# Attention in twelve steps instead of sixteen: two query blocks share a step in a two-block transformer kernel

## The chip, the cores and the metric

The kernel runs on one core of one Trainium2 chip. Times are device microseconds (us) of one execution. TensorE is written PE (its weight loads PEld), VectorE DVE, ScalarE ACT, GpSimd POOL, SyncE SP.

## What is computed

Two transformer blocks follow each other on 512 tokens of width 1024, in float32. There are three attentions, each with 8 heads of width 64: A (chunked, with a relative bias) and B (stick-breaking) in the first block, F (forgetting) in the second. Cut to what the change touches:

```python
# A: softmax over keys of (q.k * scale + bias), mask by chunks of 64
scores = einsum('bnqhd,bnkhd->bnhqk', qc, kb) * (dh ** -0.5)
probs = softmax(where(valid, scores + bias, -inf));  out = probs @ vb
# B: per query block of 128, causal
log_keep = where(causal, -softplus(z), 0.0)
log_after = lax.cumsum(log_keep, axis=3, reverse=True) - log_keep
w = where(causal, exp(log_sigmoid(z) + log_after), 0.0);  out = w @ vh
# F: per query block of 128, causal
s = q @ k.T * scale + c[:, :, t0:t1, None] - c[:, :, None, :t1]
out = softmax(where(mask, s, -inf)) @ v
```

Around them stand the projections, gates, a gated feed-forward in each block and some smaller pieces. Query block qb (0 to 3, 128 queries each) sees the first qb + 1 key blocks of 128: its scores are 128, 256, 384 or 512 columns wide.

## The kernel before

**The projections** are the bulk. Every weight matrix is read in slots of 128 rows by 512 columns. SP loads a slot into `w_raw`, ACT copies it to a rounded `w_hi` (L862), POOL makes the rest `w_lo` (L661), eight slots ahead of PE, and PE multiplies it: 4 tiles of 3 matmuls of 512 columns each (L1650). A group is 4 or 8 slots (k) that add up in banks 0 to 3, one bank for each tile. At a group's last slot the tiles end one after the other, and each is then *taken* out of its bank, mostly by DVE (`take_dve`, such as L1118 for kB, L1123 for a gate, L1136 for branchA and branchH). The next group's first slot waits for that, tile by tile (`tile_taken`).

**Attention** runs between slots on banks 4 to 7. Heads go in four pairs; a pair had four steps, one for each query block, so a branch had STEPS = 16. Each branch also has LAG = 2 steps more, and one after them. Step i is issued by each engine at its own place in one common list, SCHEDULE, which is walked by every engine in the same order. In step i

- PE (`att_pe`) makes the scores of step i for both heads into banks 4 and 5 (L1560), if a pair is finished its 16 products with the values into bank 6 (L1575, 'PV'), and the transposes of the probabilities of step i - 2 into banks 6 and 7 (L1587), two for each key block.
- DVE (`att_dve`) for A and F makes the reciprocal of step i - 1, then waits until the transposes of step i - 2 are through, since the scores' copy in `work` goes into the buffer that they read (`ring_free`), and then, for each head, adds the mask (F: L1222), adds the bias and finds the maximum (A: L1212, F: L1224, 'reduce'). Each of these is linked: the next waits for its end. Last it copies transposes out of their banks (L1231; A both units, B and F the first, ACT the second at L782).
- for B, DVE makes the reverse cumulative product of step i - 1 (L1189, 'scan', after a memset of one column) and adds the mask (L1206), ACT makes two sigmoids for each head (L770, L771), and POOL multiplies the two (L709).
- ACT (`att_act`) for A and F scales the probabilities of step i - 1 (L761) and makes the exponentials (L779).

Where the steps stand is computed by `attention(kind, first, last)` in `make_schedule`: step i gets a share of the slots first to last in proportion to `room`, which was block + 5. A step stands behind its slot, and behind the take of a group if that slot is the group's last. Here 'gateH1.6' means group 1 of gateH behind its slot 6 (slots count from 0), and A9 is step 9 of attention A.

Of the kernel before, what the change touches and what calls it, by code (L numbers as in the profile page):

```python
# [23 lines left out]
P = 128  # L24
# [17 lines left out]
STEPS = TB * PAIRS  # L42
# [72 lines left out]
def make_schedule():  # L115
# [90 lines left out]

def transposed(i):

    if not 0 <= i < STEPS:
        return ()  # L210
    return (1,) if i % TB < 2 else (0, 1)
# [108 lines left out]
def two_block_kernel(nc, a, out):  # L320
    ctx = ExitStack()
    with ctx:
# [326 lines left out]
        def _(e):  # L649
# [25 lines left out]
            for x in SCHEDULE:  # L675
# [60 lines left out]
        def transposes_out(e, kind, i, unit, copy):  # L736

            a_, c = A[kind], i % TB + 1
            pair, q = i // TB, slice((c - 1) * P, c * P)
# [4 lines left out]
            if c <= 2:  # L744
                o = probs_t[kind][:, :, 0:c, q]
                copy(o, ps[b][:, 0:2 * c * P].rearrange("p (h c t) -> p h c t", h=2, c=c)).then_inc(bank_free[b], 1)
            else:
                o = probs_t[kind][:, unit, 0:c, q]
                copy(o, ps[b][:, 0:c * P].rearrange("p (c t) -> p c t", c=c)).then_inc(bank_free[b], 1)

        def att_act(e, kind, i):

            a_ = A[kind]
            n = (i % TB + 1) * P
            if 1 <= i <= STEPS and kind != "B":
# [18 lines left out]
            elif i < STEPS:  # L774
                k = 0 if kind == "A" else 1
                for j in (2 * i, 2 * i + 1):
                    ring = work[j % 4][:, 0:n]
                    e.wait_ge(a_["s_ready"], j + 1)
                    e.activation(ring, ring, ACT.Exp, scale=-1.0,  # L779
                                 bias=mneg[:, k, j:j + 1], accum_out=rsum[:, k, j:j + 1]).then_inc(a_["e_ready"], 1)  # L780
# [392 lines left out]
        def att_dve(e, kind, i, link):  # L1173

            a_ = A[kind]
            n = (i % TB + 1) * P
            if finished_pair(i - 1) is not None:
                outputs_rest(e, kind, finished_pair(i - 1), link)
            if 1 <= i <= STEPS and kind == "B":
                m = ((i - 1) % TB + 1) * P  # L1180
                for h in range(2):
                    j = 2 * i - 2 + h
                    e.wait_ge(a_["keep_ready"], j + 1)
                    if i > 1:
                        e.wait_ge(a_["p_ready"], j - 1)
                    k_, o_ = keep[h], after[h]
                    link(e.memset(o_[:, m - 1:m], 1.0))
                    rev = lambda t, lo_, hi_: t[:, hi_ - 1:(lo_ - 1 if lo_ else None):-1]
                    e.tensor_tensor_scan(rev(o_, 0, m - 1), rev(k_, 1, m), rev(k_, 1, m), 1.0,  # L1189
                                         ALU.mult, ALU.bypass).then_inc(a_["after_ready"], 1)  # L1190
            elif 1 <= i <= STEPS:
                k = 0 if kind == "A" else 1
                e.wait_ge(a_["e_ready"], 2 * i)
                e.reciprocal(rinv[:, k, 2 * i - 2:2 * i], rsum[:, k, 2 * i - 2:2 * i]).then_inc(a_["r_ready"], 1)
            if i < STEPS:
                if kind != "B":
                    ring_free(e, kind, i)
                for h in range(2):
                    j = 2 * i + h
                    head = 2 * (i // TB) + h  # L1200
                    ring = work[j % 4]
                    b, use = USE[("sc", kind, j)]
                    e.wait_ge(a_["sc_done"], j + 1)
                    if kind == "B":
                        d = ps[b][:, n - P:n]
                        e.tensor_tensor(d, d, strict[:, :], ALU.add).then_inc(a_["s_ready"], 1)  # L1206
                    elif kind == "A":
                        if j == 0:

                            e.wait_ge(bias_full, 16)  # L1210
                            link(e.tensor_scalar(bias_mask[64:128, :, S - 64:S], bias_mask[64:128, :, S - 64:S], NEG, None, ALU.add))
                        link(e.tensor_tensor_reduce(out=ring[:, 0:n], in0=ps[b][:, 0:n], in1=bias_mask[:, head, S - n:S],  # L1212
                                                    scale=-1.0, scalar=3e38, op0=ALU.add, op1=ALU.min,
                                                    accum_out=mneg[:, 0, j:j + 1]))
                        e.nop().then_inc(bank_free[b], 1)
                        e.nop().then_inc(a_["s_ready"], 1)
                    else:

                        if j == 0:
                            e.wait_ge(ff["rows"], 16)  # L1220
# [321 lines left out]
        def att_pe(e, kind, i):  # L1542
# [3 lines left out]
            if i < STEPS:  # L1546
                pair, qb = divmod(i, TB)
# [8 lines left out]
                n = (qb + 1) * P  # L1556
                banks = [bank_wait(e, ("sc", kind, 2 * i + h)) for h in range(2)]
                for h in range(2):
                    r = slice(64 * h, 64 * h + 64)
                    e.matmul(banks[h][:, 0:n], qk1[qn][r, pair, qb * P:n], qk1[kn][r, pair, 0:n],  # L1560
                             start=True, stop=True).then_inc(a_["sc_done"], 1)
            pair = finished_pair(i)
            if pair is not None:
# [4 lines left out]
                last = TB * pair + TB - 1  # L1568
# [323 lines left out]
```

## Time and profile before

| | us |
|---|---|
| median of 3 runs | 1579.41 (1578.83 to 1580.74) |
| the profiled execution | 1579.64 |
| its span, first to last instruction | 1577.9 |
| PE busy | 1565.9 (99%) |
| POOL busy | 754.7 (48%) |
| ACT busy | 693.4 (44%) |
| DVE busy | 642.9 (41%) |

The span is what the profile shows between the first and the last instruction; 1.7 us of the execution lie around it. A matmul's busy time overlaps that of the next, so what a matmul costs is read from the starts: one start to the next. The three attentions lie at 93 to 193 us (A), 200 to 316 us (B) and 971 to 1088 us (F).

### The profile page before, as it was taken

What the parts mean: (1) busy time and instruction counts of PE and PEld (TensorE: products, weight loads), DVE (VectorE), ACT (ScalarE), POOL (GpSimd) and SP (SyncE); (2) the same over time, 40 slices, a digit from 0 to 9 for tenths busy, and PEclk for the clock granted to TensorE, in tenths of its full rate; (3) what the DMA queues carried; (4) which work ended last, traced back from release to release, by engine and by line L of the source; (5) the groups of instructions that cost most, each with busy time, mean ns of one, the idle gap of its engine ahead of it and who ended that gap; (6) DMA issues with size and microseconds to landing.
All of it is one profiled execution on the core that took longest, in us unless ns stands there. A gap on an engine that the chain in (4) does not pass through costs nothing.

```text
span 1577.9 us, 23446 instructions
## 1 busy us (share of the span) xinstructions
PE 1565.9 (99%) x8030; PEld 1256.7 (80%) x8030; DVE 642.9 (41%) x1075; ACT 693.4 (44%) x1196; POOL 754.7 (48%) x585
## 2 busy tenths in 40 slices
PE   8999999999999999999999999999999999999999
PEld 7876777788888888888877887768888888888887
DVE  5334356444355444220477543543342122210234
ACT  5555455433544444332543644655453333322342
POOL 6632365644644554444578434323544444444441
PEclk9999999999999999999999999999999999999999
DMA  5422222223323333333232323222333333332331
GB/s 184 143 80 61 74 74 60 75 81 87 112 83 99 106 100 93 100 100 88 80 88 76 93 69 132 69 67 74 101 94 100 100 93 100 107 100 94 97 96 61
DMA packets 103352, 145.60 MB, mean 92 GB/s; under 512 B 11109, under 2 KB 57166, under 8 KB 103134
## 3 DMA queue, kind: packets, MB, share of 16 engines
q1 hardware_dynamic: 103102, 142.30, 30.3%
q10 hardware_dynamic: 160, 2.11, 0.3%
q8 instruction: 55, 0.90, 0.2%
q14 instruction: 35, 0.29, 0.1%
HBM read 142.24 MB, written 2.13 MB: 91 GB/s over the span
## 4 chain that ended last, share of the span: by engine, by line
PE 95%; DVE 2%; ACT 1%; issue 1%; POOL 1%; DMA 1%; SPq 0%; DVEq 0%; ACTq 0%; POOLq 0%
PE bank L1650 86%; PE bank L1560 2%; PE bank L1587 2%; PE bank L1575 2%; POOL w_lo L661 1%; DMA xtok<-in_x 0%; PE bank L1805 0%; PE bank L1636 0%; ACT L869 0%; PE bank L1828 0%; PE bank L1845 0%; ACT hE L1046 0%; PE bank L1781 0%; PE bank L1839 0%; PE bank L1866 0%
## 5 line engine op out<-in xcount | busy, mean ns | idle before, releaser
L661 POOL TENSOR_TENSOR w_lo<-w_raw,w_hi 128x512 fp32r<-128x512 f32 x516 | 695.7, 1357 | 782.2 <-ACT w_hi L862 781.5
L862 ACT ACTIVATE w_hi<-w_raw 128x512 fp32r<-128x512 f32 x516 | 319.0, 628 | 651.1 <-PE bank L1650 579.1
L1650 PE MATMUL bank<-h_hi,w_lo 128*128 128x512 f32 x1244 | 490.0, 394 | 0.8 <-ACT hv L981 0.7
L1650 PE MATMUL bank<-h_hi,w_hi 128*128 128x512 f32 x1244 | 484.6, 390 | 0.0
L1650 PE MATMUL bank<-h_lo,w_hi 128*128 128x512 f32 x1244 | 484.1, 389 | 0.0
L1650 PEld LDWEIGHTS bank<-h_hi,w_lo 128*128 128x128 f32 x1244 | 233.5, 188 | 51.1 <-issue 2.3
L1650 PEld LDWEIGHTS bank<-h_hi,w_hi 128*128 128x128 f32 x1244 | 233.5, 188 | 49.3
L1650 PEld LDWEIGHTS bank<-h_lo,w_hi 128*128 128x128 f32 x1244 | 233.7, 188 | 46.9
L1245 DVE TENSOR_TENSOR bank<-bank,rstd 128x512 f32<-128x512 f32 x88 | 60.1, 700 | 261.6 <-PE bank L1650 261.6
L1650 PE MATMUL bank<-g_hi,w_lo 128*128 128x512 f32 x352 | 137.0, 389 | 0.0
L1650 PE MATMUL bank<-g_hi,w_hi 128*128 128x512 f32 x352 | 136.9, 389 | 0.0
L1650 PE MATMUL bank<-g_lo,w_hi 128*128 128x512 f32 x352 | 136.9, 389 | 0.0
L1144 DVE TENSOR_TENSOR xT<-bank,xT 128x512 f32<-128x512 f32 x32 | 22.0, 688 | 206.5 <-PE bank L1650 204.5
L1650 PEld LDWEIGHTS bank<-g_hi,w_hi 128*128 128x128 f32 x352 | 66.1, 188 | 13.8
L1650 PEld LDWEIGHTS bank<-g_hi,w_lo 128*128 128x128 f32 x352 | 66.1, 188 | 13.7
L1650 PEld LDWEIGHTS bank<-g_lo,w_hi 128*128 128x128 f32 x352 | 66.1, 188 | 13.6
L1650 PE MATMUL bank<-w_lo,h_hi 128*128 128x512 f32 x184 | 73.6, 400 | 0.4 <-DVE fk L1118 0.4
L1650 PE MATMUL bank<-w_hi,h_hi 128*128 128x512 f32 x184 | 71.9, 391 | 0.0
L1650 PE MATMUL bank<-w_hi,h_lo 128*128 128x512 f32 x184 | 71.7, 390 | 0.0
L1254 DVE SCALAR_TENSOR_TENSOR acc<-bank,vec,acc 128x511 f32<-128x511 f32 x88 | 62.9, 746 | 13.2 <-ACT acc L817 8.1
L779 ACT ACTIVATE work<-work,mneg 128x128 f32<-128x128 f32 (+3 forms) x64 | 36.0, 562 | 32.7 <-DVEq L1228 17.1
L1650 PE MATMUL bank<-mix_hi,w_hi 128*128 128x512 f32 x128 | 49.8, 389 | 0.0
(297 smaller groups left out, 1781.0 us busy)
## 6 DMA issues: line engine op xcount, KB each, us to landing
w_raw<-in_w_in SPq DMA_DIRECT2D x168, 256.0 KB
w_raw<-in_w_ffn_up SPq DMA_DIRECT2D x88, 256.0 KB
w_raw<-in_w_ffn_down SPq DMA_DIRECT2D x88, 256.0 KB
w_raw<-in_w_ffn_gate SPq DMA_DIRECT2D x88, 128.0 KB
w_raw<-in_w_ffn_up SPq DMA_DIRECT2D x88, 128.0 KB
w_raw<-in_w_out SPq DMA_DIRECT2D x32, 256.0 KB
w_raw<-in_w_branch_a SPq DMA_DIRECT2D x16, 256.0 KB
w_raw<-in_w_branch_b SPq DMA_DIRECT2D x16, 256.0 KB
```

The lines of the kernel that those rows point to most:

```text
L661: e.tensor_tensor(w_lo[:, pos % SPLIT_SLOTS, :], w_raw[:, pos % RAW_SLOTS, :], w_hi[:, pos % SPLIT_SLOTS, :].bitcast(F32), ALU.subtract).t ...
L779: e.activation(ring, ring, ACT.Exp, scale=-1.0, bias=mneg[:, k, j:j + 1], accum_out=rsum[:, k, j:j + 1]).then_inc(a_["e_ready"], 1)
L862: e.activation(w_hi[:, pos % SPLIT_SLOTS, :], w_raw[:, r, :], ACT.Copy).then_inc(hi_full, 1)
L1144: e.tensor_tensor(xT[:, j, :], bank, xT[:, j, :], ALU.add).then_inc(x_ready, 1)
L1245: e.tensor_tensor(ps[banks + n][:, :], ps[banks + n][:, :], rstd[:, :], ALU.mult).then_inc(q["scaled"], 1)
L1254: e.scalar_tensor_tensor(out=o, in0=ps[banks + n][:, 0:S - shift], scalar=vec[:, conv_col(tap, col, n // 2)], in1=o, op0=ALU.mult, op1=ALU ...
L1560: e.matmul(banks[h][:, 0:n], qk1[qn][r, pair, qb * P:n], qk1[kn][r, pair, 0:n], start=True, stop=True).then_inc(a_["sc_done"], 1)
L1575: mm = e.matmul(bank[64 * h:64 * h + 64, c * P:S], vtok[vn][:, c, d], probs_t[kind][:, h, c, c * P:S], start=c == 0, stop=c == TB - 1, ski ...
L1587: mm = e.transpose(bank[:, o:o + P], work[(2 * j + h) % 4][:, c * P:(c + 1) * P], ident[:, :])
L1650: mm = e.matmul(ps[banks + n][:, :], l, r, start=k == 0 and i == 0, stop=k == p.kc - 1 and i == 2)
```

## The change

Query blocks 0 and 2 of a pair of heads now go in one step, of 128 + 384 = 512 columns in one bank; blocks 1 and 3 go alone. The order in a pair is block 1, blocks 0 and 2, block 3. A branch has 12 steps. What DVE and ACT did once for a head and a block is still done for each piece in A and F; the semaphores count steps. In B the sigmoids and POOL's product go over both pieces in one instruction, and the scans stay one for each piece. The `room` of the three kinds of step is 6, 9 and 8, over the same slots first to last.

```diff
-STEPS = TB * PAIRS
+BLOCKS = ((1,), (0, 2), (3,))
+PARTS = len(BLOCKS)
+STEPS = PARTS * PAIRS
...
-        room = [min(i, STEPS - 1) % TB + 5 for i in range(STEPS + LAG + 1)]
+        room = [(6, 9, 8)[min(i, STEPS - 1) % PARTS] for i in range(STEPS + LAG + 1)]
...
+def pieces(i):
+
+    at, said = 0, []
+    for qb in BLOCKS[i % PARTS]:
+        said.append((qb, at, (qb + 1) * P))
+        at += (qb + 1) * P
+    return said
+
+
+def width(i):
+    return sum(n for _, _, n in pieces(i))
...
-    return (1,) if i % TB < 2 else (0, 1)
+    return (1,) if width(i) <= 2 * P else (0, 1)
...
-                    link(e.memset(o_[:, m - 1:m], 1.0))
-                    rev = lambda t, lo_, hi_: t[:, hi_ - 1:(lo_ - 1 if lo_ else None):-1]
-                    e.tensor_tensor_scan(rev(o_, 0, m - 1), rev(k_, 1, m), rev(k_, 1, m), 1.0,
-                                         ALU.mult, ALU.bypass).then_inc(a_["after_ready"], 1)
+                    for qb, at, m in pieces(i - 1):
+                        k_, o_ = keep[h][:, at:at + m], after[h][:, at:at + m]
+                        link(e.memset(o_[:, m - 1:m], 1.0))
+                        ins = e.tensor_tensor_scan(o_[:, m - 2::-1], k_[:, m - 1:0:-1], k_[:, m - 1:0:-1], 1.0, ALU.mult, ALU.bypass)
+                    ins.then_inc(a_["after_ready"], 1)
...
+                    for qb, at, m in pieces(i):
+
+                        k, bias = (0, bias_mask[:, head, S - m:S]) if kind == "A" else (1, c_rows[:, head, 0:m])
+                        j = statistic(i, qb, h)
+                        link(e.tensor_tensor_reduce(out=ring[:, at:at + m], in0=ps[b][:, at:at + m], in1=bias,
                                                     scale=-1.0, scalar=3e38, op0=ALU.add, op1=ALU.min,
-                                                    accum_out=mneg[:, 0, j:j + 1]))
...
+                                                    accum_out=mneg[:, k, j:j + 1]))
+                    e.nop().then_inc(bank_free[b], 1)
+                    e.nop().then_inc(a_["s_ready"], 1)
...
-                for h in range(2):
-                    r = slice(64 * h, 64 * h + 64)
-                    e.matmul(banks[h][:, 0:n], qk1[qn][r, pair, qb * P:n], qk1[kn][r, pair, 0:n],
-                             start=True, stop=True).then_inc(a_["sc_done"], 1)
+                for qb, at, n in pieces(i):
+                    for h in range(2):
+                        r = slice(64 * h, 64 * h + 64)
+                        mm = e.matmul(banks[h][:, at:at + n], qk1[qn][r, pair, qb * P:n], qk1[kn][r, pair, 0:n],
+                                      start=True, stop=True)
+                        if qb == BLOCKS[i % PARTS][-1]:
+                            mm.then_inc(a_["sc_done"], 1)
```

The steps also land at other slots. On PE before, at the end of group kB (slot kB0.7) and the start of vB, where step A10 with its PV stood between the two:

```order
L1650 MATMUL bank<-h_hi,w_hi 128x512
L1560 MATMUL bank<-kA,qA 128x384 [waits bank_free5,bank_free4]
L1560 MATMUL bank<-kA,qA 128x384
L1575 MATMUL bank<-probs_tA,vA 64x512 [waits bank_free7,bank_free6]
L1575 MATMUL bank<-probs_tA,vA 64x512
L1575 MATMUL bank<-probs_tA,vA 64x384 x2
L1575 MATMUL bank<-probs_tA,vA 64x256 x2
L1575 MATMUL bank<-probs_tA,vA 64x128 x2
L1587 MATMUL bank<-ident,work_78 128x128 [waits p_readyA,bank_free7]
L1587 MATMUL bank<-ident,work_79 128x128
L1650 MATMUL bank<-w_lo,h_hi 128x512 [waits taken_dve,lo_full]
```

The same place on PE now (L1678 is what L1650 was):

```order
L1678 MATMUL bank<-h_hi,w_lo 128x512
L1678 MATMUL bank<-h_lo,w_hi 128x512
L1678 MATMUL bank<-h_hi,w_hi 128x512
L1678 MATMUL bank<-w_lo,h_hi 128x512 [waits taken_dve,lo_full]
L1678 MATMUL bank<-w_hi,h_lo 128x512
```

The step between the groups is gone: vB's first matmul, which waits for DVE's take of kB, follows kB's last one. On DVE before, the last step ahead of that take (A9, behind kB0.6) and the take, L1118; the ISA rows are the reduces and their readouts:

```order
L1212 ISA work_80,mneg<-bank,bias_mask 128x256 [waits sc_doneA,tr_doneA]
L1212 ISA mneg 128x1
L1212 ISA work_81,mneg<-bank,bias_mask 128x256 [waits dve_seq,sc_doneA]
L1212 ISA mneg 128x1
L1231 COPY probs_tA<-bank 128x4x128 [waits dve_seq,pv_doneA,tr_doneA]
L1231 COPY probs_tA<-bank 128x4x128 [waits pv_doneA,tr_doneA]
L1118 TENSOR_TENSOR kB<-bank,rstd 128x512 [waits rstd_ready,tile_done] x4
```

And on DVE now, where step A7 stands behind the same slot:

```order
L1250 ISA work_80,mneg<-bank,bias_mask 128x128 [waits sc_doneA,tr_doneA]
L1250 ISA mneg 128x1
L1250 ISA work_80,mneg<-bank,bias_mask 128x384 [waits dve_seq]
L1250 ISA mneg 128x1
L1250 ISA work_81,mneg<-bank,bias_mask 128x128 [waits dve_seq,sc_doneA]
L1250 ISA mneg 128x1
L1250 ISA work_81,mneg<-bank,bias_mask 128x384 [waits dve_seq]
L1250 ISA mneg 128x1
L1257 COPY probs_tA<-bank 128x4x128 [waits dve_seq,pv_doneA,tr_doneA]
L1257 COPY probs_tA<-bank 128x4x128 [waits pv_doneA,tr_doneA]
L1146 TENSOR_TENSOR kB<-bank,rstd 128x512 [waits rstd_ready,tile_done] x4
```

Two reduces became four in front of the take. In F, on DVE before, step F9 stands behind branchH1.2, ahead of the take of branchH group 1 (L1136):

```order
L1222 TENSOR_TENSOR bank<-bank,causal 128x128 [waits sc_doneF,tr_doneF]
L1224 ISA work_80,mneg<-bank,c_rows 128x256 [waits dve_seq]
L1224 ISA mneg 128x1
L1222 TENSOR_TENSOR bank<-bank,causal 128x128 [waits dve_seq,sc_doneF]
L1224 ISA work_81,mneg<-bank,c_rows 128x256 [waits dve_seq]
L1224 ISA mneg 128x1
L1231 COPY probs_tF<-bank 128x4x128 [waits dve_seq,pv_doneF,tr_doneF]
L1136 TENSOR_TENSOR gateH_121<-bank,gateH_121 128x512 [waits curved_gateH,tile_done] x4
```

Now step F7 is there:

```order
L1241 TENSOR_TENSOR bank<-bank,causal 128x128
L1250 ISA work_80,mneg<-bank,c_rows 128x128 [waits dve_seq]
L1250 ISA mneg 128x1
L1250 ISA work_80,mneg<-bank,c_rows 128x384 [waits dve_seq]
L1250 ISA mneg 128x1
L1241 TENSOR_TENSOR bank<-bank,causal 128x128 [waits dve_seq,sc_doneF]
L1241 TENSOR_TENSOR bank<-bank,causal 128x128
L1250 ISA work_81,mneg<-bank,c_rows 128x128 [waits dve_seq]
L1250 ISA mneg 128x1
L1250 ISA work_81,mneg<-bank,c_rows 128x384 [waits dve_seq]
L1250 ISA mneg 128x1
L1257 COPY probs_tF<-bank 128x4x128 [waits dve_seq,pv_doneF,tr_doneF]
```

Four masks and four reduces stand where two and two stood, ahead of the same take. Where the steps stand that come last before a group's end, and whether a step stands between the take and the next group:

| end of group | before | now |
|---|---|---|
| kB | A9 behind slot 6 (256 wide), then A10 between | A7 behind slot 6 (128 + 384), none between |
| vB | A15 behind 6, A16 between | A11 behind 5, A12 between |
| gateA 0 | B1 behind 6, B2 between | B1 behind 6 (128 + 384), none between |
| branchA 1 | B10 behind 1, B11 between | B8 behind 2 (512, PV), none between |
| gateH 1 | F4 behind 6 (128), F5 between | F3 behind 6 (256), none between |
| branchH 0 | F6 behind 1 (PV), F7 between | F5 behind 2 (512, PV), none between |
| branchH 1 | F9 behind 2 (256), F10 between | F7 behind 2 (128 + 384), none between |

## Rows read from the trace of the kernel before

**Rows 1.** The page: PE's busy time, and its granted clock in 40 slices.

```profile
PE 1565.9 (99%) x8030; PEld 1256.7 (80%) x8030; DVE 642.9 (41%) x1075; ACT 693.4 (44%) x1196; POOL 754.7 (48%) x585
...
PEclk9999999999999999999999999999999999999999
```

**Rows 2.** Waits of PE: who was waited for, us in total, times, longest.

```profile
PE bank L1805 <- issue: 2.4, 1, 2.4
...
PE bank L1587 <- POOL work L709: 0.6, 1, 0.6
```

**Rows 3.** Timeline, PE at step A0: start us, duration us, instruction, [idle before].

```profile
92.16 0.39 PE L1650 MATMUL bank<-h_hi,w_hi 128*128 128x512 f32 x1
...
92.84 0.39 PE L1650 MATMUL bank<-h_hi,w_hi 128*128 128x512 f32 x1
93.16 0.49 PE L1560 MATMUL bank<-kA,qA 64*128 64x128 f32 x4
93.58 0.50 PE L1650 MATMUL bank<-h_hi,w_lo 128*128 128x512 f32 x1
```

**Rows 4.** Timeline, PE at step A3, 512 columns and four transposes.

```profile
103.78 0.39 PE L1650 MATMUL bank<-h_hi,w_hi 128*128 128x512 f32 x1
104.09 1.13 PE L1560 MATMUL bank<-kA,qA 64*128 64x512 f32 x4
105.15 0.66 PE L1587 MATMUL bank<-ident,work 128*128 128x128 f32 x4
105.57 0.47 PE L1650 MATMUL bank<-h_hi,w_lo 128*128 128x512 f32 x1
105.88 0.39 PE L1650 MATMUL bank<-h_lo,w_hi 128*128 128x512 f32 x1
```

**Rows 5.** Timeline, PE: the PV of pair 0 of A.

```profile
120.48 2.37 PE L1575 MATMUL bank<-probs_tA,vA 128*64 128x512 f32 x16
```

**Rows 6.** Timeline, DVE's reduces of 384 columns in A6, then of 128 in A12.

```profile
123.26 0.56 DVE L1212 CUSTOM_DVE_ANT_0 work<-bank,bias_mask 128x384 f32<-128x384 f32 x1 [3.52 <-PE bank L1587]
...
124.11 0.56 DVE L1212 CUSTOM_DVE_ANT_0 work<-bank,bias_mask 128x384 f32<-128x384 f32 x1 [0.29 <-DVE mneg L1212]
...
158.63 0.47 PE L1650 MATMUL bank<-w_lo,h_hi 128*128 128x512 f32 x1
158.91 0.29 DVE L1212 CUSTOM_DVE_ANT_0 work<-bank,bias_mask 128x128 f32<-128x128 f32 x1 [3.83 <-PE bank L1587]
...
159.49 0.29 DVE L1212 CUSTOM_DVE_ANT_0 work<-bank,bias_mask 128x128 f32<-128x128 f32 x1 [0.28 <-DVE mneg L1212]
```

**Rows 7.** Timeline at the end of group vB, steps A15 and A16.

```profile
176.45 0.47 PE L1650 MATMUL bank<-w_lo,h_hi 128*128 128x512 f32 x1
...
179.30 0.81 PE L1587 MATMUL bank<-ident,work 128*128 128x128 f32 x6
179.32 1.25 ACT L981 ACTIVATE vB<-bank,rtok 128x512 f32<-128x512 f32 x2
...
180.13 0.47 PE L1650 MATMUL bank<-h_hi,w_lo 128*128 128x512 f32 x1
```

**Rows 8.** Timeline, DVE in F9 (256 columns) and the take of branchH group 1.

```profile
1024.90 0.30 DVE L1222 TENSOR_TENSOR bank<-bank,causal 128x128 f32<-128x128 f32 x1 [1.97 <-PE bank L1587]
...
1025.91 0.30 DVE L1222 TENSOR_TENSOR bank<-bank,causal 128x128 f32<-128x128 f32 x1 [0.24 <-DVE mneg L1224]
...
1027.00 0.69 DVE L1231 COPY probs_tF<-bank 128x512 f32<-128x512 f32 x1 [0.32 <-DVE mneg L1224]
...
1027.61 0.68 DVE L1136 TENSOR_TENSOR gateH<-bank,gateH 128x512 f32<-128x512 f32 x1
```

**Rows 9.** Timeline, DVE's takes of fk and the matmul that waited for the first.

```profile
910.44 1.88 DVE L1118 TENSOR_TENSOR fk<-bank,rstd 128x512 f32<-128x512 f32 x3
...
911.27 0.47 PE L1650 MATMUL bank<-w_lo,h_hi 128*128 128x512 f32 x1 [0.40 <-DVE fk L1118]
```

**Rows 10.** One line's instructions, B's scans: durations ns least/median/most, first and last start.

```profile
L1189 DVE TENSOR_TENSOR_SCAN after<-keep x32: 421/1132/2106, 202.6 to 303.2; 128x127 f32<-128x127 f32 x8, 128x255 f32<-128x255 f32 x8, 128x383 f32<-128x383 f32 x8, 128x511 f32<-128x511 f32 x8
```

More of the change, by code:

```diff
@@ L736, in transposes_out @@
         def transposes_out(e, kind, i, unit, copy):
-            a_, c = A[kind], i % TB + 1
-            pair, q = i // TB, slice((c - 1) * P, c * P)
+            a_ = A[kind]
+            pair = i // PARTS
             b, use = USE[("pt", kind, i, unit)]
@@ L743, in transposes_out @@
                 e.wait_ge(a_["pv_done"], pair)
[L744 to L749, printed above, removed]
+            for qb, at, n in pieces(i):
+                q, c = slice(qb * P, (qb + 1) * P), qb + 1
+                if len(transposed(i)) == 1:
+                    ins = copy(probs_t[kind][:, :, 0:c, q], ps[b][:, 0:2 * n].rearrange("p (h c t) -> p h c t", h=2, c=c))
+                else:
+                    ins = copy(probs_t[kind][:, unit, 0:c, q], ps[b][:, at:at + n].rearrange("p (c t) -> p c t", c=c))
+            ins.then_inc(bank_free[b], 1)
         def att_act(e, kind, i):
             a_ = A[kind]
-            n = (i % TB + 1) * P
+            n = width(i)
             if 1 <= i <= STEPS and kind != "B":
@@ L758, in att_act @@
                 e.wait_ge(a_["r_ready"], i)
-                for j in (2 * i - 2, 2 * i - 1):
-                    ring = work[j % 4][:, 0:((i - 1) % TB + 1) * P]
-                    e.activation(ring, ring, ACT.Copy, scale=rinv[:, k, j:j + 1]).then_inc(a_["p_ready"], 1)
+                for h in range(2):
+                    for qb, at, m in pieces(i - 1):
+                        j = statistic(i - 1, qb, h)
+                        ring = work[(2 * i - 2 + h) % 4][:, at:at + m]
+                        ins = e.activation(ring, ring, ACT.Copy, scale=rinv[:, k, j:j + 1])
+                    ins.then_inc(a_["p_ready"], 1)
             if i < STEPS and kind == "B":
@@ L775, in att_act @@
                 k = 0 if kind == "A" else 1
[L776 to L780, printed above, removed]
+                for h in range(2):
+                    e.wait_ge(a_["s_ready"], 2 * i + h + 1)
+                    for qb, at, m in pieces(i):
+                        j = statistic(i, qb, h)
+                        ring = work[(2 * i + h) % 4][:, at:at + m]
+                        ins = e.activation(ring, ring, ACT.Exp, scale=-1.0,
+                                           bias=mneg[:, k, j:j + 1], accum_out=rsum[:, k, j:j + 1])
+                    ins.then_inc(a_["e_ready"], 1)
             if kind != "A" and len(transposed(i - LAG)) == 2:
@@ L1175, in att_dve @@
             a_ = A[kind]
-            n = (i % TB + 1) * P
             if finished_pair(i - 1) is not None:
@@ L1193, in att_dve @@
                 e.wait_ge(a_["e_ready"], 2 * i)
-                e.reciprocal(rinv[:, k, 2 * i - 2:2 * i], rsum[:, k, 2 * i - 2:2 * i]).then_inc(a_["r_ready"], 1)
+                for qb, at, m in pieces(i - 1):
+                    j = statistic(i - 1, qb, 0)
+                    ins = e.reciprocal(rinv[:, k, j:j + 2], rsum[:, k, j:j + 2])
+                ins.then_inc(a_["r_ready"], 1)
             if i < STEPS:
@@ new lines, in att_dve @@
+                    head = 2 * (i // PARTS) + h
+                    ring = work[(2 * i + h) % 4]
+                    b, use = USE[("sc", kind, 2 * i + h)]
+                    e.wait_ge(a_["sc_done"], 2 * i + h + 1)
+                    if kind == "A" and i == 0 and h == 0:
+                        e.wait_ge(bias_full, 16)
+                        link(e.tensor_scalar(bias_mask[64:128, :, S - 64:S], bias_mask[64:128, :, S - 64:S], NEG, None, ALU.add))
+                    if kind == "F" and i == 0 and h == 0:
+                        e.wait_ge(ff["rows"], 16)
@@ L1546, in att_pe @@
             if i < STEPS:
-                pair, qb = divmod(i, TB)
+                pair = i // PARTS
                 if i == 0:
@@ L1567, in att_pe @@
                     tile_taken(e, vn, 0, 3)
-                last = TB * pair + TB - 1
+                last = PARTS * pair + PARTS - 1
                 for unit in transposed(last):
```

58 lines of the change are left out of this document (23 added, 35 removed).

## The prediction

> **What bounds the kernel.** I read the page first: PE is busy 99% of the span at a full granted clock in every slice [rows 1]. Then the waits of PE: it waits for almost nothing, and in the attentions for POOL alone, once, 0.6 us [rows 2]. So the time is PE's stream of instructions. Faster work on DVE, ACT or POOL gives nothing; only fewer or cheaper PE instructions give time, and only a new wait of PE takes it. The columns that PE streams do not change: the same scores, PV and transposes. Two questions are left: what a step costs PE beside its columns, and where PE now meets something that is late.
>
> **What a step costs PE.** In the stream a matmul follows the last after 0.227 us (92.16 to 92.84 us is three of them) [rows 3]. Scores take 0.42 us for 128 columns of both heads [rows 3] and 1.06 for 512 [rows 4], which is 0.213 for each 128 columns and 0.21 for the group. Four transposes take 0.42 [rows 4]. The step in rows 4 puts 105.88 - 103.78 = 2.10 us between two stream matmuls that are two places apart: less two pitches (0.45), 512 score columns (0.85) and the transposes (0.42), 0.38 are left. That is the price of breaking into the stream and coming back, weights exposed and all. I take 0.375. Four steps fewer in each of three branches: 12 x 0.375 = **4.5 us saved**.
>
> Does the second pair of scores in a merged step bring its own fixed cost? PV shows not: 16 records take 2.37 us [rows 5], and its columns, 512 + 384 + 256 + 128 for both heads, are ten times 128, so 2.13; 0.24 is left for sixteen, as against 1.13 - 0.85 = 0.28 for four [rows 4]. [...]
>
> **Old waits that go.** POOL's 0.6 us [rows 2] is at step B13, one slot behind B12, with 512-wide products of POOL to wait for. Now only B7 stands one slot behind a step that makes such products, and its scores are 512 wide instead of 256, which gives POOL 0.43 us more. I count the 0.6 as gone. At the end of vB six transposes last 0.83 us to the next matmul (179.30 to 180.13) [rows 7] where six are worth 0.63: PE waited 0.2 for the take of tile 0, though A16 stood between. A11 is now a slot earlier and A12 still stands between: gone. Together **0.8 saved**.
>
> **New waits.** The next group's first matmul waits for the take of the last group's tile 0. After a step, PE's slot takes 2.85 us (176.45 to 179.30) [rows 7], and that is when it wants the bank, if no step stands between. DVE comes to the take only after its own part of the step, and for A and F that part starts after PE's: 0.28 us behind the first matmul of the slot (158.63 to 158.91) [rows 6]. Call the start of that slot S; a take is 0.69 long [rows 8] and PE starts 0.14 after its end (910.44 + 0.69 to 911.27) [rows 9].
>
> - A7 behind kB0.6. From start to start a reduce of 128 takes 0.58, one of 384 takes 0.85 [rows 6]. Two heads: 2.86. Two copies, 0.61 each (1027.00 to 1027.61) [rows 8]: 1.22. S + 0.28 + 2.86 + 1.22 + 0.69 + 0.14 = S + 5.2; PE wants it at 2.85: **2.35**.
> - F3 behind gateH1.6. A head of 256 columns is 1.01, the last 1.09 [rows 8]; the copy now goes in two pieces, 0.61 + 0.15 for the second's fixed part (0.29 us for 128 columns, 0.56 for 384 [rows 6] leave 0.15 at no columns): S + 0.28 + 2.10 + 0.76 + 0.83 = S + 3.97: **1.1**.
> - F5 behind branchH0.2. A head of 512 is 0.27 more than 256 (same slope): 1.28 + 1.36. S + 0.28 + 2.64 + 0.61 + 0.83 = S + 4.36: **1.5**.
> - F7 behind branchH1.2. A head has two masks and two reduces: 1.15 for mask and reduce of 384 (1.01 and half of 0.27), 0.58 for the other reduce, about 0.27 for the other mask: 2.0, twice. S + 0.28 + 4.05 + 0.61 + 0.83 = S + 5.8: **2.9**.
>
> The takes of the later tiles follow at 0.69 each, and PE's tiles at 3 x 0.227 = 0.68, so no more is lost there. Sum **7.9 us**. Before, each of these ends had a step of PE between take and next group or a much narrower one ahead of it, which is why the waits show nothing. B1 and B8 also stand uncovered before a take, but DVE's part of B, the scans, belongs to the step before and needs nothing of PE's current step; I count 0, at most 1 each.
>
> **Where the cover is thin.** In F4, ACT copies the second unit of transposes out about when F5's PV wants the bank; and at gateA0.5 and 0.6, B1's scores wait for four sigmoids that are 128 columns wider. I count 0 for both, at most 0.5 each. Merged sigmoids and products save ACT and POOL time that nobody waits for: 0.
>
> **Sum.** On the profiled execution, 1579.64 us (0.2 over the median): 1579.64 - 4.5 - 0.8 + 7.9 = 1582.2; against the median **1582.0**, 0.16% more. A measurement of this kernel tells a change from none at about 0.2%, or 3.2 us.
>
> **Rivals.**
> 1. Saving alone (0.08). The takes are not late, since DVE is elsewhere faster than its rows or since the order lets it in: 1579.4 - 5.3 = 1574.1. For it: DVE is idle 59% of the time. Against: A15's take was late even with a step between [rows 7], and it is queue order, not load, that delays it.
> 2. Some of the four (0.13). One or two of the four waits are absent or half as long: about 1576.5 to 1580.
> 3. B turns slow, the other side (0.15). In B a chain goes round: scans (DVE), product (POOL), the next step's scans. Scans of 127 to 511 columns take 0.42 to 2.11 us [rows 10]. The merged step has four scans instead of two, for each head one short and one long. If a step's scans come to more than the gap to the next step (about 7 us at two slots), DVE's masks, then ACT's banks, then PE's scores are late. It decides where the short piece costs some 1.3 us instead of 0.42: then the step has 1.8 us more, in four pairs up to 7, of which the gaps of three slots swallow about half: 1582.0 + 3.5 = 1585.5. The Trainium skill (GPSIMD Engine Reference, 1. Specifications) says that POOL shares its memory interface with VectorE and that they contend where VectorE has two SBUF inputs, as the scan has; the spread in rows 10 would fit.
> 4. The clock (0.04). A wait of 2.9 us is longer than any before. PE once stood idle 2.4 us [rows 2] and the granted clock stayed at 2.4 GHz in that slice [rows 1]. If it fell to 1.2 GHz for a slot, the 12 matmuls would cost 2.7 us more: 1585 or so.
>
> **Numbers.** The forecast holds 0.60: 1580.0 to 1584.0, with the thin covers and two rows' worth of error in DVE's parts; three fifths of it, 0.36, lie under 1582.6, the edge of 0.2%. Same: 0.36 and the 0.13 of rival 2, near 0.50. Slower: 0.24, 0.15 and 0.04, near 0.42. Faster: 0.08. For the range I cut rival 1 and the top of rivals 3 and 4: 1577.0 to 1586.0.
>
> **What would show it.** Waits of PE: L1678 for DVE's kB, gateH (twice by L1151 and L1164) with 1 to 3 us each, in all about 8. In the timeline, PE idle between the last matmul of kB and the first of vB, about 2.3 us. A merged step with eight transposes puts about 2.1 us (0.85 + 0.85 + 0.38) into the stream. Wrong would be: no such waits (rival 1), PE waiting at L1586 or L1615 in B (rival 3), a granted clock under full in the slices of the attentions (rival 4), or a merged step that costs more than its columns and 0.38.

## The result, and the profile after

| | before | after |
|---|---|---|
| median of 7 runs, us | 1579.46 (1578.83 to 1580.86) | 1584.65 (1583.69 to 1586.33) |
| the profiled execution, us | 1579.64 | 1584.28 |
| its span, us | 1577.9 | 1582.6 |

The ratio is 1.0032, 95% interval 1.0023 to 1.0041: the changed kernel is 5.2 us slower (3.6 to 6.5), more than the 0.2% that can be told from no change. The forecast of 1582.0 had the sign but half of the size, the time lies inside the range of 1577.0 to 1586.0, and "same", to which the prediction gave the most, is not what happened.

The page after, PE's busy time and its granted clock, answers [rows 1]:

```profile
PE 1562.9 (99%) x8030; PEld 1257.4 (79%) x8030; DVE 639.7 (40%) x1079; ACT 690.5 (44%) x1188; POOL 753.2 (48%) x577
...
PEclk9999999999999999999999999999999999999999
```

PE is busy 3 us less in a span that is 4.7 us longer, although a stretch at a lower clock (see e4) adds 1.7 us to its busy time. So the saving came, and new idle time took it and more. The waits of PE after (who was waited for, us in total, times, longest) answer [rows 2]:

```profile
PE bank L1615 <- DVEq L1198: 2.9, 2, 1.5
PE bank L1833 <- issue: 2.8, 2, 2.4
PE bank L1678 <- DVE gateH L1164: 2.1, 1, 2.1
PE bank L1678 <- DVE kB L1146: 1.7, 1, 1.7
PE bank L1678 <- POOL w_lo L682: 1.4, 1, 1.4
...
PE bank L1678 <- DVE gateH L1151: 0.8, 1, 0.8
```

Four of these are the forecast waits for a take. L1146 is kB behind A7, L1151 gateH1 behind F3, L1164 branchH1 behind F7. The one named POOL w_lo is the take of branchH0 behind F5: DVE's take starts at 1013.97, PE goes on at 1014.80, 0.83 later as [rows 9] have it, and a product of POOL only happened to end at the same time. From start to start of the matmuls on both sides, less the pitch of 0.227, the four cost 1.88, 0.97, 1.51 and 2.30 us. The first line was not forecast: PE waits in L1615, the transposes, for the release of a bank by DVE, 1.5 us at A12 and 1.4 us at B12.

What a step costs is read as the prediction did for [rows 4]: from the stream matmul before it to the second one behind it, less two pitches of 0.227. I call that "added" below. A merged step, A7 in the timeline after (start, duration, instruction):

```profile
137.29 0.39 PE L1678 MATMUL bank<-h_hi,w_hi 128*128 128x512 f32 x1
137.61 1.14 PE L1586 MATMUL bank<-kA,qA 64*128 64x128 f32 x8
138.68 1.09 PE L1615 MATMUL bank<-ident,work 128*128 128x128 f32 x8
139.53 0.48 PE L1678 MATMUL bank<-h_hi,w_lo 128*128 128x512 f32 x1
139.84 0.39 PE L1678 MATMUL bank<-h_lo,w_hi 128*128 128x512 f32 x1
```

139.84 - 137.29 - 0.45 = 2.10 us, which is what the prediction gave. Over all steps of the three attentions, the added time is 99.47 us before and 97.13 after, the latter with 3.34 us of waiting at A12 and B12.

### The profile page after: what moved, and what is told of

It reads as the page before. It is cut to its first block, busy times and chain, and to the rows that moved or that the text cites. A ratio compares the mean times of both kernels' runs of the same rounds, so it can differ in the third digit from the quotient of the medians.

```text
span 1582.6 us, 23329 instructions
## 1 busy us (share of the span) xinstructions
PE 1562.9 (99%) x8030; PEld 1257.4 (79%) x8030; DVE 639.7 (40%) x1079; ACT 690.5 (44%) x1188; POOL 753.2 (48%) x577
## 4 chain that ended last, share of the span: by engine, by line
PE 94%; DVE 2%; ACT 1%; issue 1%; POOL 1%; DMA 1%; SPq 0%; DVEq 0%; ACTq 0%
PE bank L1678 85%; PE bank L1586 2%; PE bank L1615 2%; PE bank L1603 2%; POOL w_lo L682 1%; PE bank L1833 0%; DMA xtok<-in_x 0%; DVE work L1250 0%; PE bank L1664 0%; ACT L897 0%; PE bank L1856 0%; PE bank L1873 0%; ACT hE L1074 0%; PE bank L1809 0%; ACT gateH L990 0%
## 5 line engine op out<-in xcount | busy, mean ns | idle before, releaser
L1678 PE MATMUL bank<-h_hi,w_lo 128*128 128x512 f32 x1244 | 489.9, 394 | 2.9 <-DVE gateH L1164 2.1
L1678 PE MATMUL bank<-h_lo,w_hi 128*128 128x512 f32 x1244 | 484.9, 390 | 0.0
L1678 PE MATMUL bank<-h_hi,w_hi 128*128 128x512 f32 x1244 | 484.9, 390 | 0.0
L1678 PEld LDWEIGHTS bank<-h_hi,w_lo 128*128 128x128 f32 x1244 | 233.9, 188 | 55.2 <-issue 6.3
L1678 PEld LDWEIGHTS bank<-h_hi,w_hi 128*128 128x128 f32 x1244 | 233.9, 188 | 49.4
L1678 PEld LDWEIGHTS bank<-h_lo,w_hi 128*128 128x128 f32 x1244 | 234.1, 188 | 47.0
L1678 PE MATMUL bank<-g_hi,w_lo 128*128 128x512 f32 x352 | 137.0, 389 | 0.0
L1678 PE MATMUL bank<-g_hi,w_hi 128*128 128x512 f32 x352 | 136.9, 389 | 0.0
L1678 PE MATMUL bank<-g_lo,w_hi 128*128 128x512 f32 x352 | 136.9, 389 | 0.0
L1678 PEld LDWEIGHTS bank<-g_lo,w_hi 128*128 128x128 f32 x352 | 66.1, 188 | 13.8
L1678 PEld LDWEIGHTS bank<-g_hi,w_lo 128*128 128x128 f32 x352 | 66.1, 188 | 13.7
L1678 PEld LDWEIGHTS bank<-g_hi,w_hi 128*128 128x128 f32 x352 | 66.1, 188 | 13.6
L1678 PE MATMUL bank<-w_lo,h_hi 128*128 128x512 f32 x184 | 73.5, 399 | 2.1 <-DVE kB L1146 1.7
L1678 PE MATMUL bank<-w_hi,h_hi 128*128 128x512 f32 x184 | 71.8, 390 | 0.0
L1678 PE MATMUL bank<-w_hi,h_lo 128*128 128x512 f32 x184 | 71.7, 390 | 0.0
L806 ACT ACTIVATE work<-work,mneg 128x128 f32<-128x128 f32 (+2 forms) x64 | 35.7, 559 | 39.3 <-DVEq L1254 38.3
L1678 PE MATMUL bank<-mix_hi,w_lo 128*128 128x512 f32 x128 | 49.8, 389 | 0.0
```

The source lines that it names most:

```text
L806: ins = e.activation(ring, ring, ACT.Exp, scale=-1.0, bias=mneg[:, k, j:j + 1], accum_out=rsum[:, k, j:j + 1])
L1678: mm = e.matmul(ps[banks + n][:, :], l, r, start=k == 0 and i == 0, stop=k == p.kc - 1 and i == 2)
```

## The experiments

All but one of the variants only move steps: a table of (attention, step): slot goes ahead of the computed slots in `attention`. The "slot" is the index in the run's list of slots, as `behind` counts it. What the step does is unchanged. Where a fence below is from such a variant, its line numbers are one higher than after's (or before's), and in e7 up to three.

```diff
-        return [(first + sum(room[:i]) * (last - first + 1) // sum(room), ("att", kind, i))
+        moved = {...}
+        return [(moved.get((kind, i), first + sum(room[:i]) * (last - first + 1) // sum(room)), ("att", kind, i))
```

The theory: the loss is four uncovered takes (6.66 us), a slow clock behind the last (about 1.7 us in the profiled execution) and two waits for the bank of the PV output (3.34 us), against a saving of under 6 us.

**e1, all of it moved away.**

```diff
+        moved = {("A", 7): 37, ("F", 3): 55, ("F", 4): 57, ("F", 5): 59, ("F", 6): 61, ("F", 7): 63, ("F", 8): 65,
+                 ("A", 12): 48, ("A", 13): 50, ("A", 14): 52, ("B", 12): 80, ("B", 13): 82, ("B", 14): 84}
```

> The changed kernel with 13 of its attention steps one or two slots later: A7 and F3 to F8, so that a step stands between the last quarter of kB, gateH1, branchH0, branchH1 and the stream behind them, and A12 to A14 and B12 to B14, so that A12 and B12 don't stand right behind the end of vB and of gateB0. Theory (the loss is made of four uncovered takes, 1.88 + 0.97 + 1.51 + 2.30 = 6.66 us, of about 1.7 us at a granted clock of 0.5 behind the last of them, and of two waits for the bank of the PV output, 1.71 + 1.65 = 3.36 us, beside a saving of about 5.85 us): all of it goes, 1584.65 - 6.66 - 1.7 - 3.36 = 1572.9 us; from the kernel before, 1579.46 - 5.85 = 1573.6 us. So 1572.5 to 1574.5, ratio to before 0.9958 to 0.9968. Rival (the waits only move, since VectorE and GpSimd are late with other work wherever the steps stand): 1577 or more. In the trace: none of the PE waits for the takes of kB, gateH and branchH at L1679, nor the ones of 1.5 us for L1199 at L1616, and no granted clock under 1 near 1032 us.

Measured: 1573.37 us beside 1579.82 for before, ratio 0.9959 (0.9946 to 0.9973). As the theory had it. This version is faster than both kernels, 6.4 us faster than the one before. Twelve of the thirteen steps stand one slot later. A7 stands one slot earlier (37 instead of 38), which the expectation has wrong: no step stands between kB and vB here either, but DVE is through with A7's part when the take comes. In its trace PE waits for nothing between 60 and 320 us, and between 900 and 1100 us only for this, which before has too [rows 9]:

```profile
PE bank L1679 <- DVE fk L1147: 0.4, 1, 0.4
```

Its steps add 93.79 us, 5.68 less than before.

**e2, the takes alone.**

```diff
+        moved = {("A", 7): 37, ("F", 3): 55, ("F", 4): 57, ("F", 5): 59, ("F", 6): 61, ("F", 7): 63, ("F", 8): 65}
```

> The changed kernel with A7 and F3 to F8 later, A12 to A14 and B12 to B14 as they were. Theory: the four uncovered takes (6.66 us) and the slow clock behind the last (about 1.7 us) go, the two waits for the PV output's bank stay: 1584.65 - 8.4 = 1576.3 us, or e1 + 3.4 us. Rival (bank waits cost nothing, the whole loss is in the takes): equal to e1.

Measured: 1576.59 us, 0.9982 (0.9973 to 0.9991). It is 3.2 us above e1 where 3.4 were expected, and the two waits for L1199 are in its trace at 1.50 and 1.44 us. So the bank costs what its waits show.

**e3, the bank alone.**

```diff
+        moved = {("A", 12): 48, ("A", 13): 50, ("A", 14): 52, ("B", 12): 80, ("B", 13): 82, ("B", 14): 84}
```

> The changed kernel with A12 to A14 and B12 to B14 one slot later alone, the takes of kB, gateH1, branchH0 and branchH1 still uncovered. Theory: PE no longer waits 1.5 us for L1199 (yA_lo, yB_lo) at A12 and B12: 1584.65 - 3.4 = 1581.3 us. Rival (those two waits are only PE being ahead of VectorE, and come back at the next step of the same queue): 1584 to 1585.

Measured: 1581.55 us, 1.0009 (1.0000 to 1.0018), against 1584.65 and 1.0032 for after: 3.1 us by the medians. The four takes wait as in after (excess 1.88, 0.97, 1.51, 2.31). The two causes add up: e2 and e3 each give back their own part, e1 both.

**e4, F7 alone, for the clock.** Behind F7's wait the kernel after loses more than the wait. Its timeline, PE and one line of DVE:

```profile
1029.39 0.39 PE L1678 MATMUL bank<-yH_hi,w_hi 128*128 128x512 f32 x1
...
1031.10 2.47 DVE L1164 TENSOR_TENSOR gateH<-bank,gateH 128x512 f32<-128x512 f32 x4
1031.93 0.71 PE L1678 MATMUL bank<-h_hi,w_lo 128*128 128x512 f32 x1 [2.14 <-DVE gateH L1164]
1032.43 0.63 PE L1678 MATMUL bank<-h_lo,w_hi 128*128 128x512 f32 x1
1032.86 0.63 PE L1678 MATMUL bank<-h_hi,w_hi 128*128 128x512 f32 x1
...
1034.99 0.59 PE L1678 MATMUL bank<-h_lo,w_hi 128*128 128x512 f32 x1
1035.42 0.39 PE L1678 MATMUL bank<-h_hi,w_hi 128*128 128x512 f32 x1
```

From 1032.43 to 1035.42 the pitch is 0.427 instead of 0.227 for seven matmuls, and 0.50 for the one ahead: 7 x 0.2 + 0.28 = 1.7 us. The busy times by stretch (us, PE busy, the granted clock, DMA) say why: the clock granted was 0.50, so 1.2 GHz.

```profile
1030.00:1032.00 2.00, 0.07 (x1) 1.00 0.02 4
1032.00:1034.00 2.00, 2.00 (x5) 0.50 0.03 8
1034.00:1036.00 2.00, 2.00 (x7) 0.65 0.46 125
```

```diff
+        moved = {("F", 7): 63, ("F", 8): 65}
```

> The changed kernel with F7 and F8 one slot later alone, so that only the 2.30 us wait at the end of branchH1 goes. It tells whether the granted clock of 0.5 between 1032 and 1035.4 us hangs on that wait. Theory (it does): 1584.65 - 2.30 - 1.7 = 1580.6 us, and every row of windows near 1032 us shows a granted clock of 1. Rival (the clock falls there for another reason): 1584.65 - 2.3 = 1582.3 us, with the slow stretch still in the trace. The two lie 0.11% apart, so the trace decides and the time only supports.

Measured: 1581.86 us, 1.0012 (1.0003 to 1.0021). That is 2.8 us below after by the medians and 3.2 by the ratios, of which 2.30 is the wait; 0.5 to 0.9 is left for the clock, between theory and rival. A clock that does not fall every time would give that, and the traces show such a clock: e3 has the same wait, 2.15 us, in the same place, and its stretches there, the wait in the first, are

```profile
1030.00:1032.00 2.00, 1.25 (x6) 1.00 0.02 4
1032.00:1034.00 2.00, 2.00 (x10) 1.00 0.22 26
```

And in e4's own profile, where PE waited 2.22 us for DVE's `h_lo`, up to 29.23 us (1.1 us or less there in the other traces), the clock falls at that place (the same columns):

```profile
26.00:28.00 2.00, 1.00 (x5) 1.00 0.53 155
28.00:30.00 2.00, 0.78 (x3) 0.89 0.59 168
30.00:32.00 2.00, 2.00 (x6) 0.50 0.63 171
32.00:34.00 2.00, 2.00 (x8) 0.76 0.59 173
```

**e5, only F7 left uncovered.** F6, F7 and F8 stand as in after, all else as in e1.

```diff
+        moved = {("A", 7): 37, ("F", 3): 55, ("F", 4): 57, ("F", 5): 59, ("F", 6): 60, ("F", 8): 64,
+                 ("A", 12): 48, ("A", 13): 50, ("A", 14): 52, ("B", 12): 80, ("B", 13): 82, ("B", 14): 84}
```

> As e1, but F6, F7 and F8 stand where the change puts them (branchH1.0, branchH1.2, gateF0.0), so that of all new waits only the one at the end of branchH1 is left, in a kernel without any other. Theory: that take costs 2.30 us, and the granted clock falls to 0.5 behind such a wait in some executions and not in others (of nine waits of PE of 2.1 to 2.5 us in the six traces so far, five had it behind them; of the shorter ones, 1.35 to 1.72 us, none): e1 + 2.3 + 0 to 1.7 us, 1575.7 to 1577.4 us, likeliest 1576.5 beside an e1 of 1573.4. Rival (the wait is paid back later, because DVE and ACT catch up): within 1 us of e1.

Measured: 1578.62 us, 0.9990 (0.9981 to 0.9999): 5.2 us above e1, over the top of what was expected. F7's wait is there (2.31) with the slow clock behind it (0.50 from 1026 to 1028 us), but the rest was a wait that I had made myself by putting F6 one slot behind F5. Timeline of e5:

```profile
1010.32 0.70 PE L1587 MATMUL bank<-fk,fq 64*128 64x256 f32 x4
...
1010.90 0.58 ACT L817 ACTIVATE yF_hi<-bank 128x512 fp32r<-128x512 f32 x1
...
1011.51 0.69 DVE L1197 TENSOR_TENSOR yF_lo<-bank,yF_hi 128x512 fp32r<-128x512 f32 x1 [0.51 <-ACT yF_hi L817]
...
1012.32 1.09 PE L1616 MATMUL bank<-ident,work 128*128 128x128 f32 x8 [1.29 <-DVEq L1199]
```

F5 has a PV, and F6 transposes a merged step. Those transposes need bank 6, where F5's output lies until ACT has made `yF_hi` and DVE `yF_lo`. So it is the wait of A12 again, here with ACT's part in it and no take at all. 2.3 for F7 and 1.35 for F6 leave 1.6 of the 5.2 for the clock; the profiled execution lost 1.7 behind F7.

**e6, the kernel before, uncovered.**

```diff
+        moved = {("A", 10): 40, ("A", 11): 41, ("F", 5): 56, ("F", 10): 64}
```

> The kernel before, nothing merged, with A10, A11, F5 and F10 one slot later, so that no step stands between the takes of kB, gateH1 and branchH1 and the stream behind them. Theory (what costs is the missing cover, whatever the width of a step): at kB DVE comes to the take at 144.185 in the trace of before, so PE goes on at 144.185 + 0.68 + 0.14 = 145.0, and wants to at 141.24 + 2.85 = 144.09: 0.9 us; at gateH1 995.46 + 0.82 - 992.95 - 2.85 = 0.5 us; at branchH1 1027.61 + 0.82 - 1024.62 - 2.85 = 0.95 us. Sum 2.35: 1579.8 + 2.35 = 1582.2 us. Rival (only the double width of the merged steps makes the takes late): 1579.8 us, none of these waits.

Measured: 1582.46 us beside 1579.90, 1.0016 (1.0007 to 1.0025): 2.6 us where 2.35 were expected. The waits of PE between 60 and 1100 us, those of the three takes:

```profile
PE bank L1651 <- DVE gateH L1137: 0.8, 1, 0.8
PE bank L1651 <- DVE kB L1119: 0.8, 1, 0.8
...
PE bank L1651 <- DVE gateH L1124: 0.3, 1, 0.3
```

From start to start they are 0.97, 0.94 and 0.49 against the 0.95, 0.9 and 0.5 that were worked out. So no merging is needed for this loss: a step between a take and the next group covers it, and the width of the last step ahead of the take sets how much there is to cover.

**e7, the bank released ahead of the take.** Positions as in e2; DVE's order alone is changed.

```diff
                 elif what == "take":
+                    if x[1:3] in (("vB", 0), ("gateB", 0)):
+                        outputs_rest(e, x[1][-1] if x[1] == "gateB" else "A", finished_pair(11), link)
                     take_dve(e, *x[1:], link)
...
-            if finished_pair(i - 1) is not None:
+            if finished_pair(i - 1) is not None and (i != 12 or kind == "F"):
```

After at A12 first, in its timeline:

```profile
178.09 0.75 DVE L1154 TENSOR_SCALAR vB<-bank,rtok 128x512 f32<-128x512 f32 x1 [0.61 <-PE bank L1678]
...
178.76 0.68 DVE L1196 TENSOR_TENSOR yA_lo<-bank,yA_hi 128x512 fp32r<-128x512 f32 x1
...
179.55 1.09 PE L1615 MATMUL bank<-ident,work 128*128 128x128 f32 x8 [1.50 <-DVEq L1198]
```

PE's last matmul ahead of the step starts at 177.66 and it is ready some 0.3 us later. DVE first takes the last tile of vB, which it does behind PE's last matmul, and only then releases bank 6.

> As e2 (takes covered, A12 and B12 where the change puts them, right behind the ends of vB and gateB0), but VectorE does yA_lo and yB_lo of the third pair ahead of the take of vB and of gateB0 instead of behind it. No step moves on PE. Theory (A12 and B12 wait because the bank of the PV output is freed by an instruction queued behind the take): yA_hi is there at 175.8 us while VectorE is idle from 175.3 to 176.7, so the subtraction costs nothing there, and both waits of 1.5 us go: e2 - 3.3 = 1573.3 us, equal to e1. Rival (the waits come from the place of the steps in PE's stream, as e3 would also fit): 1576.6 us, equal to e2.

Measured: 1573.17 us, 0.9958 (0.9944 to 0.9971), equal to e1 and 3.4 us under e2. The timeline of e7:

```profile
177.29 0.69 DVE L1197 TENSOR_TENSOR yA_lo<-bank,yA_hi 128x512 fp32r<-128x512 f32 x1 [0.51 <-ACT yA_hi L817]
...
178.31 0.75 DVE L1155 TENSOR_SCALAR vB<-bank,rtok 128x512 f32<-128x512 f32 x1 [0.32 <-PE bank L1681]
...
179.38 1.04 PE L1618 MATMUL bank<-ident,work 128*128 128x128 f32 x8
```

The step stands where the change put it and waits for nothing. That settles it: the cause is the place in DVE's queue, and moving the step (e3) was one of two cures.

**e8 and e9, the old waits without the merge.** Steps of B one or two slots later in the kernel before.

e8:

```diff
+        moved = {("B", 5): 61, ("B", 13): 75, ("B", 14): 77, ("B", 15): 78, ("B", 17): 82}
```

> The kernel before, nothing merged, with B5, B13, B14, B15 and B17 one or two slots later, to take away the waits that the merge also took away in B. It tells the saved fixed costs from the old waits. The traces give 0.14 (B5) + 0.85 (B13) + 0.15 (B14) + 0.28 (B17) = 1.4 us of waits: 1579.8 - 1.4 = 1578.4 us, and e1 then lies 5 us under it. The prediction's own figure, 0.6 us for B13 alone: 1579.2 us. Rival (GpSimd is late with B's products wherever the steps stand): 1579.8 us or more.

Measured: 1579.17 us beside 1579.90, 0.9997 (0.9988 to 1.0006). Neither theory nor rival: the four waits were gone, but B16, now one slot behind B15, waited instead. PE's transposes of B16 in e8:

```profile
299.94 0.52 PE L1588 MATMUL bank<-ident,work 128*128 128x128 f32 x3 [0.44 <-POOL work L710]
300.89 0.52 PE L1588 MATMUL bank<-ident,work 128*128 128x128 f32 x3 [0.44 <-POOL work L710]
```

e9:

```diff
+        moved = {("B", 5): 61, ("B", 13): 75, ("B", 14): 76, ("B", 17): 82}
```

> As e8, with two of its five moves drawn back: nothing merged, B5, B13, B14 and B17 one slot later, B15 where it stands in the kernel before, so that B16 is again two slots behind B15. In e8 the waits at B5, B13, B14 and B17 were gone, but B16, one slot behind B15, waited 1.25 us. Theory (B waits wherever a step stands one slot behind one whose scans and products are wide, not wherever GpSimd is busy): all five waits are gone, 1579.9 - 1.4 = 1578.5 us, and no wait for L710 is in the trace. Rival (the waits move on to the next step again): 1579.2 to 1579.9 us.

Measured: 1577.71 us beside 1579.27, 0.9989 (0.9980 to 0.9998), 1.6 us less where 1.4 were expected, and no wait of PE between 190 and 320 us. Its steps add 98.04 us, 1.43 less than before's. So that part of the gain is free without the merge. What the merge alone brings is e1 against e9: 98.04 - 93.79 = 4.25 us, of which 0.25 is A16's wait for the take of vB. The ratios to before, 0.9959 and 0.9989, put 4.7 us between the two.

## Why the prediction was half right

Point by point, on the sum (us):

| term | predicted | measured |
|---|---|---|
| fixed cost of 12 steps | -4.5 | -4.0 |
| old waits | -0.8 | -1.7 |
| four uncovered takes | +7.9 | +6.7 |
| the bank of the PV output at A12, B12 | not in the sum | +3.3 |
| the clock behind F7 | 0 (rival 4, 0.04) | +0.5 to +1.7 |
| sum | +2.6 | +4.8 to +6.0; the medians: +5.2 |

- **What a step costs: right, a little too large.** A merged step costs 2.10 as forecast, and no weight load of the second pair shows: 1.14 us for eight score matmuls against 1.13 for four [rows 4]. The Trainium skill (TensorE: Matmul & The Clock Gate, Part 2: What happens when you issue a matmul) says that TensorE can pull a weight load ahead of matmuls that are still running; the 0.01 us agrees with that. But 12 x 0.375 took the cost from one kind of step. The steps that are left grew by 0.01 to 0.02 each, and 4.0 / 12 is 0.33. A finer look also shows that the price is not that of "breaking into the stream" as such. A step with transposes alone (A13 in the timeline after) adds 187.06 - 185.72 - 0.45 = 0.89 for 0.85 of columns, so next to nothing:

```profile
185.72 0.39 PE L1678 MATMUL bank<-h_hi,w_hi 128*128 128x512 f32 x1
185.96 1.03 PE L1615 MATMUL bank<-ident,work 128*128 128x128 f32 x8
...
186.75 0.48 PE L1678 MATMUL bank<-h_hi,w_lo 128*128 128x512 f32 x1
187.06 0.40 PE L1678 MATMUL bank<-h_lo,w_hi 128*128 128x512 f32 x1
```

  The fixed 0.37 to 0.42 is in steps that have scores or a PV (0.54 to 0.55 with both). All that the merge removed had scores, so it did not matter here.
- **Old waits: right in kind, mis-sized.** The 0.6 of [rows 2] is only the part for which PE's idle time has a releaser. From start to start B13 lost 0.85, and B5, B14 and B17 lost 0.14, 0.15 and 0.28, which no line of the waits shows. e9 measured them.
- **The four takes: the mechanism and the places are right, A7 and F7 too dear.** F3 (0.97 against 1.1) and F5 (1.51 against 1.5) hold. At A7 the term "from start to start a reduce of 128 takes 0.58" failed: that distance in [rows 6] contains the 0.28 us in which DVE turns from one head to the other. Inside a head the next reduce comes at once. Timeline after, DVE in A7:

```profile
139.81 0.29 DVE L1250 CUSTOM_DVE_ANT_0 work<-bank,bias_mask 128x128 f32<-128x128 f32 x1 [4.61 <-PE bank L1615]
...
140.14 0.56 DVE L1250 CUSTOM_DVE_ANT_0 work<-bank,bias_mask 128x384 f32<-128x384 f32 x1
...
140.99 0.29 DVE L1250 CUSTOM_DVE_ANT_0 work<-bank,bias_mask 128x128 f32<-128x128 f32 x1 [0.28 <-DVE mneg L1250]
...
142.21 1.29 DVE L1257 COPY probs_tA<-bank 128x512 f32<-128x512 f32 x2 [0.32 <-DVE mneg L1250]
143.42 1.88 DVE L1146 TENSOR_TENSOR kB<-bank,rstd 128x512 f32<-128x512 f32 x3
...
144.25 0.47 PE L1678 MATMUL bank<-w_lo,h_hi 128*128 128x512 f32 x1 [1.72 <-DVE kB L1146]
```

  0.33 from the first reduce to the second, so two heads take 2.40 and not 2.86, and the wait is 1.88 and not 2.35. F7 is the same, with the two masks in one go (0.50, where 0.3 and 0.27 were counted): 2.30, not 2.9.
- **What was missing: bank 6.** The prediction counted the widths of the steps but not which banks they write. A narrow step's transposes go to bank 7 alone. In the old order the step behind a PV transposed a narrow one (block 1), so the PV's output in bank 6 was never in the way. In the new order it transposes the merged one, in banks 6 and 7, and needs bank 6 back at once. The section on thin covers looked at bank 6 only from the other side (F4's transposes ahead of F5's PV, which cost nothing). e3 and e7 show that this was 3.3 us, and without it the forecast would have been near: 1584.65 - 3.3 = 1581.3, and e3 measured 1581.55 for that kernel. Some of that nearness is luck: the takes and the old waits came out 2.1 us cheaper than the sum has them, the fixed cost saved 0.5 less, and the clock filled much of the rest.
- **Rival 4, the clock, came in part.** It was given 0.04 because a longer idle time before [rows 2] had left the clock alone. One such observation was not enough (below). Its price was right for a full slot (2.7) but eight matmuls went slow, not twelve: 1.7. In the medians its share can be read four times. e4 leaves 0.5 to 0.9. After less e2 (8.1) and e3 less e1 (8.2) leave 1.4 and 1.5 beside the 6.66 of the takes, and e5 less e1 leaves 1.6; by the ratios these three leave 1.2 or 1.3.
- **Rivals 1 to 3 did not come.** All four waits are there. B's chain did not turn slow: the list of PE's waits after does not name L1586, and names L1615 only for DVE's release of bank 6, not for POOL. B1's step cost 0.14 more than A1's, and that is all, in e1 too. What rival 3 said of the scans themselves did show. One merged step of B in the timeline after, its two scans of 383 columns and POOL's work beside them:

```profile
208.98 1.48 POOL L682 TENSOR_TENSOR w_lo<-w_raw,w_hi 128x512 fp32r<-128x512 f32 x1 [1.48 <-ACT w_hi L890]
...
209.41 1.85 DVE L1215 TENSOR_TENSOR_SCAN after<-keep 128x383 f32<-128x383 f32 x1
...
211.79 0.95 DVE L1215 TENSOR_TENSOR_SCAN after<-keep 128x383 f32<-128x383 f32 x1
...
211.97 1.86 POOL L682 TENSOR_TENSOR w_lo<-w_raw,w_hi 128x512 fp32r<-128x512 f32 x1 [1.51 <-ACT w_hi L890]
```

  1.85 against 0.95, though POOL works beside both. The difference is who was first. Over the eleven traces, the 51 such scans that began with no instruction of POOL under way took 0.95 or 0.96 us, also the 33 in which POOL began one; those that began with one under way were longer by nearly what was left of it, up to 1.86. POOL's instruction is held the same way: 1.86 us here behind the scan, 1.28 where it runs alone. The Trainium skill (GPSIMD Engine Reference, 1. Specifications) states the contention; the trace agrees, with these numbers. But the four scans of this step end 4 us after they began, inside the two slots to the next step, so nobody waits.
- **The chances.** The forecast gave 0.50 to "same", as its centre lay 0.6 us under the edge of 0.2%. The errors of the terms that were in the sum come to +0.5 - 0.9 - 1.2 = -1.6 us, so they pulled towards "same"; what carried the time over the edge is the term that was missing (+3.3) and the clock (+0.5 to +1.7). That the time still lies in the range is luck in part: its upper end stood at 1586.0 for rivals 3 and 4, and most of what used that room is a wait that no rival named.

## What to carry to other kernels

Merging steps is worth the fixed cost of the removed ones (here 0.33 us each), but it moves every step's place in every queue. For each engine that releases a buffer, list what stands ahead of the release in the new order, and for each new width which banks it now writes. Where a wait shows, ask first whether the releasing instruction can go earlier in its own queue (e7), a step of independent work can stand in the gap, or the step ahead of it can go a slot earlier (both in e1): the same merge went from 0.3% slower to 0.4% faster with nothing but that. And read a wait from start to start of the waiting engine's stream; the list of waits left out more than half of the small ones here.

## What the runs showed of the hardware

The clock was the surprise. From 10 us on, PE stood idle for 2.14 to 2.46 us fifteen times in the eleven traces: three times behind F7, eleven times at the start of the hQ, hK matmuls near 820 us, and once at 27 us in e4. Ten times the granted clock was then 0.50 for 3.4 us (in e1 for 6.8), with a pitch of 0.427 in the stream; five times it stayed at 1. The same place did both: behind F7 the clock fell in after and e5 and not in e3, near 820 us in e1, e3, e4, e5, e7, e8 and e9 and not in before, after, e2 and e6. Of thirteen idle times of 1.29 to 1.72 us none was followed by a fall. In the first 10 us, where PE waits for the first input, the clock fell with waits of 2.28 us in e6, 2.17 in e7 and also 1.83 in e3, so 2.14 us is no lower limit. What decides stays open; the runs give no sign of it.

The timed runs suggest that the clock falls behind F7 more often than not. The mean granted clock of a whole execution is on record for 163 of them. It rounds to 1.000 in none of the 29 of after, e3 and e5, which have F7's wait, and in 36 of the 134 others.

What a fall costs depends on what comes next. In the stream (F7 in after and e5, 29 us in e4) it cost 1.7 us. Near 820 us it cost 1.2 to 1.6 us over the next twenty stream matmuls (2.8 in e1), but right behind them PE meets a wait for ACT's `hv`. That wait takes 0.8 to 0.9 us in before, after, e2 and e6 and is gone in the seven traces with the fall, so after sixty matmuls only 0.2 to 0.5 us are lost (1.7 in e1). The fall puts a spread of up to 1.7 us into every comparison here, which the medians of the timed runs average out only in part.
